# The second attention's scores in whole fp32, its query tiles copied from their bank at once, and its output tile begun in its last steps

## The chip, the cores and the metric

One core of a Trainium2 chip runs the whole program in one launch. The metric is the device time of an execution in microseconds (us); a kernel's time is the median of several executions. The profile names the engines PE (TensorE's matmuls; PEld is its weight loads), DVE (VectorE), ACT (ScalarE), POOL (GpSimd) and SP (SyncE, which issues most of the DMAs).

## What is computed

Three transformer blocks run one after the other over 512 positions of width 1024, in fp32: a block with differential attention, one with windowed attention, and a third block with convolution and forgetting attention. Between them stand gated feed-forward parts. The change touches the windowed attention, the kernel's second:

```python
q, k, v = jnp.split(h @ w_qkv, [Hq * d, Hq * d + Hkv * d], axis=-1)   # 16 query heads, 4 key heads, d = 64
q = apply_rope(q.reshape(B, S, Hq, d), cos, sin)
k = apply_rope(k.reshape(B, S, Hkv, d), cos, sin)
s = einsum('bnqhgd,bnchd->bnhgqc', q, band(k)) * d ** -0.5            # keys with |i - j| <= 128
e = exp(where(mask, s, -inf) - m);  pr = e / (sum(e) + exp(sink - m))
o = einsum('bnhgqc,bnchd->bnqhgd', pr, band(v));  return o @ w_o
# rope: (x1, x2) -> (x1 c - x2 s, x2 c + x1 s) on the halves of 32 of each head
```

## The kernel before

Activations lie with the features on the partitions: X has 8 chunks of 128 features by 512 positions. A weight slab is 128x1024. SP loads it, ACT rounds it to fp32r (`whi`, `high` at L1116), POOL subtracts to get the remainder (`wlo`, L540), and a product of an activation and a weight is made of three fp32r matmuls, hi by hi, hi by lo and lo by hi (`mm3`, L550). Four slabs are held in a ring.

The engines run programs of their own, each strictly in the order in which it is written out, and meet at semaphores. The second attention (kind 2) has 32 steps g: a pair of heads j = g // 4 and a block of 128 queries qb = g % 4. In step g:

- TensorE (`attention`, L871) makes the scores of step g + 2 (`scores`, L715: two heads side by side on the upper and lower 64 rows, three fp32r matmuls each of 256 or 384 columns, then masks added by matmuls), a quarter of the projection of a later query tile (`project_qk`, L670: 6 matmuls of 512 columns), the transposes of the probabilities of step g (L788), and in every second step the outputs of two steps. In steps with g % 4 = 0 the projection stands last, behind the outputs, since it opens a tile.
- ACT (L1285) makes the exponentials of step g + 1 (`exps`), copies the transposed probabilities out of their banks (`prob_high`), and every four steps takes an output tile out (`evacuate`). When a projection is done (g % 4 = 3) it makes the exchanged halves of the tile, four copies of 32 partitions out of the bank (`swap_halves`, L1205); one step later it rounds the rotated tile (`q_high`, L1216); two steps later it rounds the next weight slab (`replaced`, L1129), which starts POOL's split.
- DVE (L1839) takes the maxima of the scores of step g + 2 (`maxima`), normalises the probabilities of step g + 1 (`normalise`, whose last instructions are L1793), and between the two, in steps with g % 4 = 0, rotates the tile (`rope`, L1702: the tile in its bank by the cosines at L1712, the exchanged one by the sines at L1713, their sum at L1716), and in steps with g % 4 = 1 makes the rounding's remainder (`q_low`, L1737).

The query tiles 1 to 7 of the projection kq2 all go into bank 0 (`STAGE_BANKS`), which is given back by L1712. The scores of a new pair of heads, made in steps with g % 4 = 2, wait for the count `q_ready` that `q_low` raises. The last projection ends in step 23. The attention's output tiles are split into a rounded part and a remainder (`output_high` on ACT, `output_low` on DVE, in the steps that `OSPLIT` lists), and TensorE then multiplies them by the output weights (`tiles("o2", ...)`, L1020), the first two tiles chunk by chunk.

## Time and profile before

| what | us |
| --- | --- |
| median of three executions | 2061.38 (2059.04 to 2061.61) |
| the profiled execution: its time | 2063.4 |
| its span, first to last instruction | 2061.6 |
| PE busy | 2029.3 (98%) |
| DVE busy | 1182.7 (57%) |
| ACT busy | 934.1 (45%) |
| POOL busy | 904.6 (44%) |

The second attention runs from about 737 to 872 us of the span. A timeline row has the start, the time from the first start to the last end of what was merged, the engine, the line, the operation with the tensors it writes and reads, the shapes, the count, and in brackets the engine's idle time before it with what ended that. Matmuls are pipelined, so rows overlap: from one start to the next is what a matmul holds the engine for.

### The profile page before, as it was taken

Reading aid. Unit: us, or ns where it says so; the run is one execution under the profiler, and the core shown is the slowest. Engines: PE = TensorE matmul, PEld = TensorE weight load, DVE = VectorE, ACT = ScalarE, POOL = GpSimd, SP = SyncE. Lnnn points to the kernel's source line nnn. Section 1 sums busy time; section 2 is a strip of 40 time slices with the busy share of each in tenths; the row PEclk is TensorE's granted clock in tenths of the full one; section 3 lists DMA queues with packets and bytes.
Section 4 is the critical chain, followed back from the end, with each engine's and each line's share of the span. In section 5 each row is a group of like instructions: output and inputs, shape, how many; then the busy total and the mean of one; then the engine's idle time right before and its main releaser. Section 6 shows DMA issues by size and latency. Waiting matters only on the chain.

```text
span 2061.6 us, 28278 instructions
## 1 busy us (share of the span) xinstructions
PE 2029.3 (98%) x9822; PEld 1650.2 (80%) x9822; DVE 1182.7 (57%) x1714; ACT 934.1 (45%) x1479; POOL 904.6 (44%) x660
## 2 busy tenths in 40 slices
PE   9999999999999989899999999999999999999999
PEld 6777788888887877688888887878778788888887
DVE  7687857546276678757637267547787563213122
ACT  6455545434245467735434245444642544322221
POOL 5422235545446431145544556444224454454544
PEclk9999999999999999999999999999999999999999
DMA  4322123323233210122323333222113222233223
GB/s 163 95 74 76 52 72 97 107 93 99 95 101 113 88 66 32 32 92 82 109 96 102 94 98 115 91 83 84 40 52 102 82 92 92 88 107 99 95 95 110
DMA packets 52754, 183.18 MB, mean 89 GB/s; under 512 B 6576, under 2 KB 6832, under 8 KB 52656
## 3 DMA queue, kind: packets, MB, share of 16 engines
q1 hardware_dynamic: 51072, 177.76, 26.7%
q10 hardware_dynamic: 1584, 4.07, 0.5%
q8 instruction: 67, 1.10, 0.2%
q14 instruction: 31, 0.25, 0.0%
HBM read 176.04 MB, written 2.10 MB: 86 GB/s over the span
## 4 chain that ended last, share of the span: by engine, by line
issue 49%; POOL 30%; PE 19%; DVE 1%; POOLq 1%; DMA 0%; ACT 0%; SPq 0%; ACTq 0%
POOL wlo L540 30%; PE PS L548 19%; DVE AR L2260 0%; POOLq L538 0%; POOLq L535 0%; DMA raw<-in_weights 0%; DVE Blo L2264 0%; DVE AR L2258 0%; ACT Bhi L1578 0%; DVE sq L2258 0%; ACT whi L1119 0%; DVE X L1686 0%; POOLq L540 0%; SPq L503 0%; ACTq L1118 0%
## 5 line engine op out<-in xcount | busy, mean ns | idle before, releaser
L540 POOL TENSOR_TENSOR wlo<-raw,whi 128x512 fp32r<-128x512 f32 x656 | 904.4, 1401 | 1143.8 <-ACT whi L1119 1143.0
L548 PE MATMUL PS<-Bhi,whi 128*128 128x512 f32 x2352 | 927.2, 394 | 8.8 <-DVE AR L1712 7.2
L548 PE MATMUL PS<-Blo,whi 128*128 128x512 f32 x2352 | 916.7, 390 | 0.0
L548 PE MATMUL PS<-Bhi,wlo 128*128 128x512 f32 x2352 | 916.7, 390 | 0.0
L1119 ACT ACTIVATE whi<-raw 128x1024 fp32r<-128x1024 f32 x328 | 345.3, 1057 | 523.4 <-PE PS L548 437.2
L548 PEld LDWEIGHTS PS<-Bhi,whi 128*128 128x128 f32 x2352 | 442.2, 188 | 113.9 <-issue 19.4
L548 PEld LDWEIGHTS PS<-Bhi,wlo 128*128 128x128 f32 x2352 | 442.1, 188 | 93.7
L548 PEld LDWEIGHTS PS<-Blo,whi 128*128 128x128 f32 x2352 | 442.4, 188 | 90.0 <-issue 0.7
L1630 DVE TENSOR_TENSOR AR<-PS,R 128x512 f32<-128x512 f32 x170 | 115.3, 689 | 243.1 <-PE PS L548 231.4
L1686 DVE TENSOR_TENSOR X<-X,PS 128x512 f32<-128x512 f32 x88 | 60.2, 687 | 228.7 <-PE PS L548 228.0
L1906 DVE SCALAR_TENSOR_TENSOR AR<-AR,par_sb 128x511 f32<-128x511 f32 x88 | 116.8, 1327 | 9.1 <-ACT AR L1350 9.1
L1365 ACT ACTIVATE Bhi<-AR 128x512 f32 x66 | 41.8, 633 | 167.0 <-DVE AR L1922 167.0
L1909 DVE SCALAR_TENSOR_TENSOR AR<-AR,par_sb 128x511 f32<-128x511 f32 x88 | 106.8, 1214 | 12.9 <-DVE AR L1906 2.9
L1233 ACT ACTIVATE AR<-PS,nmax 128x512 f32<-128x512 f32 (+3 forms) x160 | 93.1, 590 | 41.7 <-DVE nmax L1752 40.5
L1350 ACT ACTIVATE AR<-AR,par_sb 128x512 f32<-128x512 f32 x88 | 70.9, 806 | 39.2 <-DVE AR L1630 39.2
L1639 DVE SCALAR_TENSOR_TENSOR Blo<-X,par_sb,Bhi 128x512 fp32r<-128x512 f32 x56 | 64.0, 1153 | 34.9 <-ACT Bhi L1145 27.5
L1926 DVE TENSOR_TENSOR Blo<-AR,Bhi 128x512 f32 x66 | 47.2, 715 | 62.2 <-ACT Bhi L1365 62.2
L1922 DVE TENSOR_TENSOR AR<-AR 128x512 f32<-128x512 f32 x66 | 56.0, 849 | 35.6 <-ACT AR L1361 27.2
L1646 DVE TENSOR_TENSOR acc<-acc,sq 128x512 f32<-128x512 f32 x56 | 73.2, 1307 | 0.0
L1361 ACT ACTIVATE AR<-AR 128x512 f32<-128x512 f32 x66 | 41.4, 628 | 49.3 <-DVE AR L1909 48.7
L1752 DVE TENSOR_REDUCE nmax<-PS 128x1 f32<-128x512 f32 (+3 forms) x96 | 54.9, 613 | 12.6 <-PE PS L548 12.3
L788 PE MATMUL PS<-constR,AR 128*128 128x128 f32 x368 | 56.4, 282 | 4.4 <-DVE AR L1793 4.2
(241 smaller groups left out, 1887.4 us busy)
## 6 DMA issues: line engine op xcount, KB each, us to landing
raw<-in_weights SPq DMA_DIRECT2D x328, 512.0 KB, 3.3
AR<-AR SPq DMA_DIRECT2D x56, 64.0 KB, 2.0
X<-in_xT ACTq DMA_DIRECT2D x4, 512.0 KB, 6.9
out<-X SPq DMA_DIRECT2D x8, 256.0 KB, 3.1
AR<-in_pT ACTq DMA_DIRECT2D x2, 512.0 KB, 4.3
par_sb<-in_parameters ACTq DMA_DIRECT2D x1, 314.0 KB, 8.6
AR<-in_positions ACTq DMA_DIRECT2D x1, 256.0 KB, 8.5
con_sb<-in_constants ACTq DMA_DIRECT2D x1, 198.5 KB, 8.3
```

Source lines behind the costliest of these rows:

```text
L540: ins = pool.tensor_tensor(wlo[:, j, c], raw[:, j % RAWS, c], f32(whi[:, j, c]), ALU.subtract)
L548: return pe.matmul(out, w, x, start=start, stop=stop)
L788: last = pe.transpose(PS[:, 2 + n % 2, k * P:k * P + P], source[:, k * P:k * P + P], ident)
L1119: act.activation(whi[:, slot, :], raw[:, slot % RAWS, :], ACT.Copy)\
L1233: act.activation(probs(kind)[:, 2 * (g % 2) + s, 0:nb * P], PS[:, score_bank(kind, n), 0:nb * P], ACT.Exp, bias=nmax[:, n % 4:n % 4 + 1], ...
L1350: act.activation(cv[:, 2 * pair + u, :], us[:, 2 * pair + u, :], ACT.Identity, scale=conv_w[:, l, 1, u, bass.ds(q, 1)], bias=conv_w[:, l, ...
L1630: tt(out, PS[:, bank, :], R[:, :], ALU.mult).then_inc(tile_free[bank], 1)
L1639: stt(chunks(Blo[b])[:, m, :], X[:, m, :], gain(name, col, m), f32(chunks(Bhi[b])[:, m, :]), ALU.mult, ALU.subtract).then_inc(x_split, 1)
L1646: tt(acc[:, :], acc[:, :], sq[:, slot, :], ALU.add).then_inc(sq_used, 1)
L1686: tt(X[:, m, :], X[:, m, :], PS[:, bank, :], ALU.add)\
L1906: own.step(stt(c[:, 1:T], x[:, 0:T - 1], conv_w[:, l, 0, u, bass.ds(q, 1)], c[:, 1:T], ALU.mult, ALU.add))
L1909: stt(c[:, 0:T - 1], x[:, 1:T], conv_w[:, l, 2, u, bass.ds(q, 1)], c[:, 0:T - 1], ALU.mult, ALU.add).then_inc(conv_done, 1)
```

## The change

Three things change in the second attention.

- Scores are one fp32 matmul per head (`qk32`) instead of three fp32r ones, as the third attention's are. The rounding `q_high` and the remainder `q_low` of its tiles go.
- ACT copies a projected tile out of its bank into SBUF as soon as it is done (`taken`), which gives the bank back; the exchanged halves are made from that copy, two copies right behind it and two in the next step behind the exponentials (`exchange`). DVE rotates from SBUF (`rotate`): two multiplications that carry the scale of the queries along, and a sum that writes the tile in fp32 and raises `q_ready`. It stands in steps with g % 4 = 1, where `q_low` stood.
- The output splits stand in steps 24 to 29 and 31 instead of 29 to 31, and TensorE makes the chunks 0 to 5 of output tile 0 in steps 26 to 31, behind the scores and ahead of the transposes. `tiles("o2", ...)` goes on with chunk 6.

```diff
-        OSPLIT = {29: (0, 1, 2), 30: (3, 4), 31: (5, 6)}
+        OSPLIT = {24: (0,), 25: (1,), 26: (2,), 27: (3,), 28: (4,), 29: (5,), 31: (6,)}
+        OPART = {26: 0, 27: 1, 28: 2, 29: 3, 30: 4, 31: 5}
...
-                    if kind == 3:
-                        mm(out, qk32[rows, b, 0, cols], qk32[rows, b, 1, keys], True, False)
+                    if kind > 1:
+                        mm(out, qk32[rows, b, 0, cols], qk32[rows, kb, 1, keys], True, False)
...
+                    if kind == 2 and g in OPART:
+                        pe.wait_ge(o_split, KC + OPART[g] + 1)
+                        tile("o2", 0, 0, chunks(Bhi[0]), chunks(Blo[0]), KC, first=OPART[g],
+                             end=OPART[g] + 1)
...
-            tiles("o2", KC, chunks(Bhi[0]), chunks(Blo[0]), KC, (o_split, 8))
+            tiles("o2", KC, chunks(Bhi[0]), chunks(Blo[0]), KC, (o_split, 8), begun=len(OPART))
...
+            def taken(t, stage="kq2"):
+                n = kq2_number(stage, t)
+                used(stage, 0, t, False)
+                bank, _ = tile_of(stage, 0, t)
+                act.wait_ge(q_ready, n - 1 if n >= QT0[2] + 2 else QT0[2])
+                act.activation(qraw[:, n % 2, :], PS[:, bank, :], ACT.Copy).then_inc(tile_free[bank], 1)
+
+            def exchange(t, halves, stage="kq2"):
+                n = kq2_number(stage, t)
+                bank, before = tile_of(stage, 0, t)
+                act.wait_ge(tile_free[bank], before + 2)
+                for half in halves:
+                    for to, of in ((0, 32), (32, 0)):
+                        to, of = to + 64 * half, of + 64 * half
+                        last = act.activation(swap[to:to + 32, n % 2, :], qraw[of:of + 32, n % 2, :], ACT.Copy)
+                if halves[-1] == 1:
+                    last.then_inc(swap_ready, 1)
...
                         exps(kind, g + 1)
+                    if kind == 2 and begun is not None:
+                        exchange(begun, (1,))
                     prob_high(kind, g)
-                    if kind < 3 and begun is not None:
+                    if kind == 1 and begun is not None:
                         q_high(*place_of(kind, begun))
...
                     if done is not None and kind == 2:
-                        swap_halves(PROJ[kind], done, place_of(kind, done)[0])
+                        taken(done)
+                        exchange(done, (0,))
...
+            def rotate(t, stage="kq2"):
+                n = kq2_number(stage, t)
+                b, which = place_of(2, t)[1:] if stage == "kq2" else (0, 1 - t)
+                x, y, factor = qraw[:, n % 2, :], swap[:, n % 2, :], (QSCALE, 1.0)[which]
+                dve.wait_ge(swap_ready, n - QT0[2] + 3)
+                own.step(stt(x, x, factor, rC, ALU.mult, ALU.mult))
+                own.step(stt(y, y, factor, rS, ALU.mult, ALU.mult))
+                own.wait()
+                tt(qk32[:, b, which, :], x, y, ALU.add).then_inc(q_ready, 1)
...
-                    if kind == 2 and begun is not None:
-                        rope(PROJ[kind], begun, place_of(kind, begun)[0])
-                    if kind < 3 and halfway is not None:
+                    if kind == 2 and halfway is not None:
+                        rotate(halfway)
+                    if kind == 1 and halfway is not None:
                         q_low(*place_of(kind, halfway))
```

The tiles ahead of the first step (`kq2a`, and tiles 0 and 1 of `kq2`) are copied, exchanged and rotated in the same way; tile 0 is rotated in step 0 and tile 1 in step 1.

## Rows read from the trace of the kernel before

**Rows 1.** The page: the span, and busy time, share and instructions of each engine.
```profile
span 2061.6 us, 28278 instructions
...
PE 2029.3 (98%) x9822; PEld 1650.2 (80%) x9822; DVE 1182.7 (57%) x1714; ACT 934.1 (45%) x1479; POOL 904.6 (44%) x660
```
**Rows 2.** Waits of PE, 740 to 872: us in total, times, the longest.
```profile
PE PS L548 <- DVE AR L1712: 7.2, 6, 2.4
PE PS L788 <- DVE AR L1793: 4.2, 5, 1.3
PE PS L548 <- DVE qklo L1739: 2.2, 2, 1.5
```
**Rows 3.** Timeline of PE: two waits of the start, and one period.
```profile
753.15 0.47 PE L548 MATMUL PS<-Bhi,whi 128*128 128x512 f32 x1 [2.35 <-DVE AR L1712]
...
759.20 0.39 PE L548 MATMUL PS<-qkhi 64*128 64x256 f32 x2 [1.48 <-DVE qklo L1739]
...
763.96 0.45 PE L548 MATMUL PS<-qkhi 64*128 64x384 f32 x2
...
786.32 0.47 PE L548 MATMUL PS<-Bhi,whi 128*128 128x512 f32 x1 [0.98 <-DVE AR L1712]
...
787.88 0.39 PE L548 MATMUL PS<-qkhi 64*128 64x256 f32 x2
...
790.85 0.39 PE L548 MATMUL PS<-qkhi 64*128 64x256 f32 x2
...
795.06 0.45 PE L548 MATMUL PS<-qkhi 64*128 64x384 f32 x2
795.34 0.34 PE L548 MATMUL PS<-qklo,qkhi 64*128 64x384 f32 x2
795.51 0.34 PE L548 MATMUL PS<-qkhi,qklo 64*128 64x384 f32 x2
795.69 0.29 PE L548 MATMUL PS<-constR 64*128 64x256 f32 x2
...
801.87 0.47 PE L548 MATMUL PS<-Bhi,whi 128*128 128x512 f32 x1 [0.97 <-DVE AR L1712]
```
**Rows 4.** Busy time by stretch: us; PE, PEld, DVE, ACT, POOL; granted clock; DMA.
```profile
848.00:872.00 24.00, 18.20 (x135) 12.79 (x135) 20.24 (x59) 19.69 (x62) 2.49 (x2) 0.84 0.08 23
```
**Rows 5.** Timeline of ACT: the exchanged halves of one tile.
```profile
798.62 2.39 ACT L1213 ACTIVATE AR<-PS 32x512 f32<-32x512 f32 x4
```
**Rows 6.** Timeline of DVE in the same period.
```profile
785.48 0.69 DVE L1712 TENSOR_TENSOR AR<-PS,AR 128x512 f32<-128x512 f32 x1 [0.45 <-ACT AR L1213]
...
786.81 0.69 DVE L1716 TENSOR_TENSOR AR<-AR 128x512 f32<-128x512 f32 x1
...
789.77 0.16 DVE L1764 TENSOR_TENSOR sdiff<-nmax,nsink 128x2 f32<-128x2 f32 x1
789.84 0.69 DVE L1739 SCALAR_TENSOR_TENSOR qklo<-AR,qkhi 128x512 fp32r<-128x512 f32 x1
...
793.86 1.20 DVE L1764 TENSOR_TENSOR sdiff<-nmax,nsink 128x2 f32<-128x2 f32 x1
```
**Rows 7.** Timeline of PE in the third attention: scores in fp32, then masks.
```profile
1445.53 0.92 PE L548 MATMUL PS<-qk 64*128 64x384 f32 x4
...
1446.46 0.23 PE L548 MATMUL PS<-constR 64*128 64x128 f32 x2
```
**Rows 8.** Timeline of POOL: the weight split of the same period.
```profile
792.53 2.52 POOL L540 TENSOR_TENSOR wlo<-raw,whi 128x512 fp32r<-128x512 f32 x2 [13.04 <-ACT whi L1119]
```
**Rows 9.** Timeline of PE: the first matmul of the output tiles and the seventh.
```profile
871.89 0.80 PE L548 MATMUL PS<-Bhi,whi 128*128 128x512 f32 x1
...
874.62 0.43 PE L548 MATMUL PS<-Bhi,whi 128*128 128x512 f32 x1
```
**Rows 10.** Timeline of DVE at the end: maxima of step 25, last normalisation.
```profile
850.67 0.75 DVE L1749 TENSOR_REDUCE nmax<-PS 128x1 f32<-128x256 f32 x2
...
868.49 0.61 DVE L1793 TENSOR_SCALAR AR<-AR,rinv 128x256 f32<-128x256 f32 x2
```

More of the change, by code:

```diff
@@ L458, in finished, with kq2_number @@
             return p[0] if p and p[1] == p[2] - 1 else None
+        def kq2_number(stage, t):
+            return QT0[2] + t + (2 if stage == "kq2" else 0)
         def probs(kind):
@@ L604, in tiles @@
             def tiles(stage, n, hi, lo, nk, ready, norm=None, lead=2, late=1,
-                      meanwhile=None, part=0):
+                      meanwhile=None, part=0, begun=0):
                 if ready is None:
@@ L616, in tiles @@
                             weights(s)
-                            outs.append(open_tile(stage, 0, j))
+                            outs.append(PS[:, tile_of(stage, 0, j)[0], :] if j == 0 and begun else
+                                        open_tile(stage, 0, j))
                         for k in ks:
+                            if j == 0 and k < begun:
+                                continue
                             if j == 0:
@@ L1208, in swap_halves @@
                 bank, _ = tile_of(stage, 0, t)
-                if n >= 2:
-                    act.wait_ge(rope_ready, n - 1)
                 for to, of in ((0, 32), (32, 0), (64, 96), (96, 64)):
@@ L1476, in _ @@
             for t in range(2):
-                swap_halves("kq2a", t, QT0[2] + t)
+                taken(t, "kq2a")
+                exchange(t, (0, 1), "kq2a")
             for t in range(2):
                 replaced("kq2a", t)
-            for t in range(2):
-                q_high(QT0[2] + t, 0, 1 - t)
             for q in range(2):
@@ L1485, in _ @@
             exps(2, 0)
-            swap_halves("kq2", 0, QT0[2] + 2)
-            q_high(*place_of(2, 0))
-            swap_halves("kq2", 1, QT0[2] + 3)
+            taken(0)
+            exchange(0, (0, 1))
+            taken(1)
+            exchange(1, (0,))
             attention(2)
@@ L1525, in head_square @@
             def head_square(t):
-                act.wait_ge(rope_ready, QT0[3] + t + 1)
+                act.wait_ge(rope_ready, QT0[2] + t + 1)
                 if t >= 2:
@@ L1705, in rope @@
                 b = n % 2
-                dve.wait_ge(swap_ready, n + 1 if n < 2 else n - QT0[2] + 3)
-                if n >= 2:
-                    dve.wait_ge(q_ready, n - 1)
-                    dve.wait_ge(qhi_ready, n - 1)
+                dve.wait_ge(swap_ready, n + 1)
                 tt(qraw[:, b, :], PS[:, bank, :], rC, ALU.mult).then_inc(tile_free[bank], 1)
@@ L2074, in _ @@
             for t in range(2):
-                rope("kq2a", t, QT0[2] + t)
-            for t in range(2):
-                q_low(QT0[2] + t, 0, 1 - t)
+                rotate(t, "kq2a")
             maxima(2, 0)
             normalise(2, 0)
-            rope("kq2", 0, QT0[2] + 2)
             attention(2)
@@ L2204, in head_norm @@
                 dve.wait_ge(hspread, t + 1)
-                dve.wait_ge(rope_ready, QT0[3] + t + 1)
+                dve.wait_ge(rope_ready, QT0[2] + t + 1)
                 stt(qk32[:, b, u, :], qraw3[:, u, :], gs[:, 1 + u:2 + u], PS[:, bank, :],
```

## The prediction, made before the changed kernel was run

> **What bounds the kernel now.** I read the page first: TensorE (PE) is busy for 2029.3 of 2061.6 us [rows 1], so only the 32 us in which it is idle, and the work that is given to it, can move the time. The execution took 2063.4 us in all, 1.8 more than its span; the median of the runs, 2061.38, lies 2.0 below it, so I work out a difference from the profiled one and add it to the median.
>
> Next I read TensorE's waits in the second attention alone. It has 32 steps g, four for each pair of heads; I call a step by g mod 4. Three kinds of wait carry nearly all of the idle time: 7.2 us in six waits for the first multiplication of the rotation (L1712), 4.2 us for the probabilities (L1793), 2.2 us in two waits for the low half of a query (L1739) [rows 2]. The six waits are one per tile: projection t+1 goes into the same bank 0 as projection t, and that bank is given back only when VectorE (DVE) has multiplied out of it, behind four partial copies on ScalarE (ACT). The timeline shows one period: the projection starts at 786.32 after 0.98 us of idle, and the next at 801.87 after 0.97 [rows 3], so a period is 15.55 us, of which 14.57 are work. Five such periods run from 763.96 to 841.7 (763.96 + 5 x 15.55) [rows 3]. Before them lies a start with one wait of 2.35 us, and behind them an end without projections (step 24 on), in which ACT and DVE lead and TensorE's clock fell for a time (granted 0.84 over 848 to 872) [rows 4].
>
> **The bank given back at once.** Now ACT copies the tile (128x512 out of the bank; 0.6 us, a quarter of the four partial copies' 2.39, since 512 columns go by either way) right after the projection. The first partial copy started at 798.62 [rows 5]; a whole copy there ends at 799.2 and TensorE wants the bank only after its scores, transposes and outputs of step 0, at 801.87 less 0.97, that is 800.9. Slack 1.7 us, so the wait goes: -0.98 in each of the five periods. ACT has one copy more and one rounding of the same size (q_high) less: even. Two of the four exchange copies (0.6 each, 2.39 for four [rows 5]) go behind the exponentials of the next step, which start 0.6 us earlier; the transposed probabilities of step 0 come some 0.6 later, and TensorE needs them two steps on.
>
> **What is late next.** The rotation moves from DVE's step 0 to its step 1, behind the maxima and in the place of q_low, and it must finish before TensorE's step 2, whose scores open the next pair of heads and wait for that query. In step 1 TensorE starts its scores at 787.88, DVE is through the maxima and starts q_low at 789.84, 1.96 later [rows 3, 6] (1.96 in four periods, 2.15 in one). q_low takes 0.69, and TensorE starts step 2 at 790.85, 2.97 after step 1: 0.3 us of slack. In its place stand three operations of 128x512. The old rotation is the nearest row: 785.48 to 786.81 plus 0.69, so 2.02 us [rows 6]. With 0.09 for the longer scores (below) the query is ready at 1.96 + 0.09 + 2.02 = 4.07 after the start of step 1 and TensorE arrives at 2.97 + 0.09 = 3.06: a wait of 1.0, with the signal's way 1.05. Nothing hides it: the scores of step 2 stand ahead of projection, transposes and outputs in TensorE's order, and DVE holds the normalisation of step 2 behind the rotation, which is needed after the projection only. One wait of 0.98 goes, one of 1.05 comes, a step later. Ends for it: 0 (if the three operations took under 1.0 together) and 1.25 (the period with 2.15).
>
> **Scores as whole fp32.** The third attention already does this: from the first score matmul of 384 columns, 1445.53, to the next mask, 1446.46, 0.93 us go by, in which one further pass (cc) lies [rows 7]. A pass of the present three takes 0.17 (795.34 to 795.51), so 0.76 for the new scores against 795.69 - 795.06 = 0.63 [rows 3]: +0.13. For 256 columns I take it by width, +0.09. A period has two of each: +0.44. TensorE does this on the path, since it is the bound there; nothing hides it. Ends: +0.26 (if the cc pass is counted at a third of 0.63) and +0.5. What the change saves is a q_high and a q_low per tile, which lie on engines that are not the bound.
>
> **A period** is then 14.57 + 0.44 + 1.05 = 16.06 against 15.55, +0.51; five give +2.6 us. Ends: -0.98 + 0.26 = -0.7 each (-3.6) and -0.98 + 0.5 + 1.25 = +0.8 each (+3.9).
>
> **The start** (to 763.96). The wait of 2.35 [rows 3] goes nearly whole: bank 0 is free at 749.2, when ACT has copied. But two steps on TensorE already waited 1.48 for a q_low, at 759.20 [rows 3], and there the whole rotation stands now, behind a second rotation's 2.0 in the step before. I follow DVE: maxima to 752.5, rotation to 754.5, normalisation to 755.5, maxima, then the second rotation from 756.9 at the earliest, so the query at 759.0. GpSimd (POOL) splits weights in this stretch, and DVE's operations on SBUF are held meanwhile (0.16 us became 1.20 at 793.86, while POOL worked from 792.53 to 795.05 [rows 6, 8]); the first split here begins about 755.1, the second about 758.3, and both fall on this chain, to 761.6 at the latest. TensorE starts that step between 0.2 earlier and 2.4 later than at 759.20; it had a further 0.35 wait behind, which goes. I take +0.9 for the start; ends -1.0 and +2.0.
>
> **The end** (step 24 on). The output splits move from steps 29 to 31 to one per step from 24, and six of the eight chunks of output tile 0 move into steps 26 to 31. The second frees 18 matmuls behind the attention. At present the first six of them ran from 871.89 to 874.62 [rows 9], 0.455 each, the rest at half of that (TensorE's lower level, 1.2 GHz, after a stretch in which it waited for one normalisation after the other): 2.7 + 12 x 0.227 = 5.5 us. In the attention their 0.7 per step lies where TensorE waits for DVE anyway. The first is a gain for ACT, which had three of them (1.6 us) ahead of the exponentials of step 31; but DVE has the low half of each, and in step 24 it now waits for ACT: exponentials, half an exchange, transposed probabilities and output_high end there about 850.9, so DVE starts the maxima of step 25 at 851.5, where it started at 850.67 [rows 10]. From there it has no pause: maxima 1.45, rotation 2.0, normalisation 1.1 and a split held by POOL up to 1.7, then 0.6, four steps of 2.5 + 0.6, one normalisation 1.0: 20.3, to 871.9, where the last normalisation now ends at 868.49 + 0.61 = 869.1 [rows 10]. So the outputs end 2.8 to 3.3 later, at 875.1 against 871.89, and 5.5 us of matmuls are gone: -2.3. If the clock falls again and the six remaining passes or the scores run at half speed I give back 1.4 (the six at 0.455 instead of 0.227). The chain waits on DVE for 4 us around step 25 with TensorE idle, so I take that: -0.9. Ends -3 and +1.5.
>
> **A rule against the change.** DVE's difference of two columns, 0.16 us at 789.77, took 1.20 at 793.86 and ended when POOL's second operation did, at 795.05 [rows 6, 8]. The Trainium skill, page "SBUF — State Buffer", section "SBUF: two separate sides", says that DVE operations with two SBUF inputs and GpSimd's share a port pair which one of them holds for a whole instruction. The trace agrees on the small operations. The old rotation had one such operation out of PSUM; of the new three all read two SBUF tiles. In the five periods POOL starts 4.65 after step 1, the rotation ends at 4.07, so by my sum they pass each other with 0.6 to spare; the rival below is the case that they don't.
>
> **Sum:** +2.6 (periods) + 0.1 (the longer scores of the last step before the end) + 0.9 (start) - 0.9 (end) = +2.7. 2061.4 + 2.7 = 2064.1; I say 2064. By the ends of its terms this case runs from 2061.4 - 3.6 - 1.0 - 3 = 2053.8 to 2061.4 + 3.9 + 2.0 + 1.5 = 2068.8; the ends won't all come together, and 2060 to 2068 is where I expect it.
>
> **Rivals.** (1) *The rotation isn't late* and no wait takes the place of the one removed. For it: a 0.3 us slack exists, and if the maxima were passed sooner or the two multiplications were shorter, all of 1.05 goes. Against it: all three old operations took 0.69, whatever they read, and the maxima stand ahead. Then five periods give 5 x (-0.98 + 0.44) = -2.7, the start -1.0, the end -2.3: -6, so 2055.4. (2) *Slower: the rotation runs into POOL's split.* It decides from the point where POOL starts less than 4.07 after step 1, that is 0.6 earlier than now, or the rotation that much later. POOL starts when ACT's weight copy ends, and that copy stands behind the transposed probabilities. Then two of the three operations take about 1.2 to 1.7 instead of 0.69, +1 to +2 per period: 5 x 1.4 on top of my sum, 2071. For it: it does happen in the start, by my own walk. Against it: what ACT has ahead of its weight copy does not get shorter. (3) *The clock falls in the periods*, because the new wait comes with less work before it: in the row before, TensorE's six matmuls lost 1.4 us at half clock [rows 9]; once per period +7, so 2071. Against it: waits of 0.98 per period left the clock at full speed, and the new ones are as long.
>
> **How the numbers follow.** A measurement of this kernel can tell about 0.2% (4 us) from no change: below 2057.3 is faster, above 2065.5 slower. My case 0.60 (same 0.41, slower 0.17, faster 0.02); rival 1 0.20 (faster 0.17, same 0.03); rivals 2 and 3 0.13 and 0.07 (slower 0.19, same 0.01). Together faster 0.19, same 0.45, slower 0.36. The range for 8 in 10 takes in half of rival 1 and half of rivals 2 and 3: 2055 to 2071.
>
> **What would show it.** In the changed profile the wait for L1712 is gone from TensorE's list, and waits for the new rotation's last addition stand there, seven or more, near 1.05 each, at the scores of step 2; the period is 16.06. Score pairs of 384 take 0.76 to the mask. The first matmul behind the last outputs comes some 3 us later after step 24 than now, and is one of chunk 6. I am wrong if the period is under 15.2 (rival 1), if the rotation's additions take over 1 us in the periods (rival 2), or if the granted clock falls between 764 and 842 (rival 3).

## The result, and the profile after

The changed kernel takes 2067.64 us in the median of 8 runs, the kernel before 2061.41 on the same chip: the ratio of their runs is 1.0033, 95% interval 1.0025 to 1.0042. By the medians that is 6.2 us slower, 3.6 above the forecast of 2064 and inside its range. The profiled execution took 2066.82 us, 1.8 more than its span.

On the page TensorE (PE) is busier by 1.8 us and the span is longer by 3.4 than in [rows 1]:

```profile
span 2065.0 us, 28121 instructions
...
PE 2031.1 (98%) x9758; PEld 1647.3 (80%) x9758; DVE 1168.9 (57%) x1704; ACT 935.7 (45%) x1479; POOL 904.4 (44%) x660
```

The span understates the loss: before the attention the profiled execution of after was 0.9 ahead, and behind it the one of before lost 1.1 on balance, with a clock fall near 1496 us (granted clock 0.83 over 1490 to 1500; 1.00 in after). So I measure between four rows that both kernels have (called the ledger below): the last update of X ahead of the attention, the sink difference of steps 6 and 26, and the first update of X from output tile 0. VectorE (DVE) rows of before:

```profile
716.57 0.69 DVE L1952 TENSOR_TENSOR X<-X,PS 128x512 f32<-128x512 f32 x1
...
769.33 0.16 DVE L1764 TENSOR_TENSOR sdiff<-nmax,nsink 128x2 f32<-128x2 f32 x1
...
847.08 0.16 DVE L1764 TENSOR_TENSOR sdiff<-nmax,nsink 128x2 f32<-128x2 f32 x1
...
883.81 0.69 DVE L1686 TENSOR_TENSOR X<-X,PS 128x512 f32<-128x512 f32 x1 [9.28 <-PE PS L548]
```

and of after:

```profile
715.66 0.69 DVE L1994 TENSOR_TENSOR X<-X,PS 128x512 f32<-128x512 f32 x1
...
774.01 0.16 DVE L1806 TENSOR_TENSOR sdiff<-nmax,nsink 128x2 f32<-128x2 f32 x1
...
853.87 0.16 DVE L1806 TENSOR_TENSOR sdiff<-nmax,nsink 128x2 f32<-128x2 f32 x1
...
888.40 0.69 DVE L1721 TENSOR_TENSOR X<-X,PS 128x512 f32<-128x512 f32 x1 [3.97 <-PE PS L554]
```

After minus before at the four: -0.91, +4.68, +6.79, +4.59. So the start costs 5.6, twenty steps (five periods) cost 2.1, the end gives back 2.2: +5.5 for the attention, of the 6.2 that the runs show. The start alone is nearly the whole loss.

TensorE's waits, 740 to 880 us (who waited, for what, by which line; us in total, times, the longest), against [rows 2]:

```profile
PE PS L554 <- DVE qk L1758: 14.6, 7, 5.8
PE PS L798 <- ACT pt L1290: 1.0, 1, 1.0
PE PS L798 <- DVE AR L1835: 0.5, 1, 0.5
```

The bank's wait is gone, and so are q_low's and most of those for the probabilities. In their place stand seven waits for the rotation's last addition (L1758), 14.6 us. TensorE's timeline has them (start, length; in brackets the idle time before and who ended it), the counterpart of [rows 3] and [rows 9]:

```profile
754.56 0.88 PE L798 MATMUL PS<-constR,AR 128*128 128x128 f32 x6 [0.51 <-DVE AR L1835]
761.20 1.22 PE L554 MATMUL PS<-qk 64*128 64x256 f32 x4 [5.76 <-DVE qk L1758]
...
768.40 0.92 PE L554 MATMUL PS<-qk 64*128 64x384 f32 x4
...
780.09 0.70 PE L554 MATMUL PS<-qk 64*128 64x256 f32 x4 [0.99 <-DVE qk L1758]
...
791.95 0.70 PE L554 MATMUL PS<-qk 64*128 64x256 f32 x4
...
796.06 0.70 PE L554 MATMUL PS<-qk 64*128 64x256 f32 x4 [1.01 <-DVE qk L1758]
...
861.50 1.22 PE L554 MATMUL PS<-qk 64*128 64x256 f32 x4 [3.77 <-DVE qk L1758]
...
881.89 0.47 PE L554 MATMUL PS<-Bhi,whi 128*128 128x512 f32 x1
```

One wait of 5.76 in the start, five of about 1.0 in the periods (796.06 less 780.09: a period is 15.97), one of 3.77 at the end. The four score matmuls of 256 columns behind the longest waits take 1.22 where those of the periods take 0.70: they ran at the lower of TensorE's two clock levels. Busy time by stretch shows the same (us; PE, PEld, DVE, ACT, POOL; granted clock; DMA), the counterpart of [rows 4]:

```profile
744.00:764.00 20.00, 13.72 (x74) 10.15 (x73) 14.73 (x35) 13.38 (x34) 5.68 (x4) 0.83 0.25 80
...
858.00:869.00 11.00, 7.50 (x39) 5.43 (x40) 9.73 (x23) 7.10 (x23) 2.62 (x2) 0.69 0.15 49
758.00:769.00 11.00, 7.80 (x38) 5.73 (x38) 6.04 (x14) 2.42 (x10) 2.60 (x2) 0.56 0.29 95
```

Over 758 to 769 the clock is 0.56, so nearly all of that stretch is at 1.2 GHz; before it was 1.00 there.

What holds the rotation in the start is on DVE and on GpSimd (POOL), the counterparts of [rows 6] and [rows 8]. DVE:

```profile
756.01 1.20 DVE L1806 TENSOR_TENSOR sdiff<-nmax,nsink 128x2 f32<-128x2 f32 x1
757.13 0.68 DVE L1755 SCALAR_TENSOR_TENSOR AR<-AR 128x512 f32<-128x512 f32 x1
757.73 1.75 DVE L1756 SCALAR_TENSOR_TENSOR AR<-AR 128x512 f32<-128x512 f32 x1
759.51 1.63 DVE L1758 TENSOR_TENSOR qk<-AR 128x512 f32<-128x512 f32 x1
...
793.99 0.68 DVE L1755 SCALAR_TENSOR_TENSOR AR<-AR 128x512 f32<-128x512 f32 x1
794.60 0.69 DVE L1756 SCALAR_TENSOR_TENSOR AR<-AR 128x512 f32<-128x512 f32 x1
795.32 0.69 DVE L1758 TENSOR_TENSOR qk<-AR 128x512 f32<-128x512 f32 x1
```

POOL:

```profile
754.59 2.60 POOL L546 TENSOR_TENSOR wlo<-raw,whi 128x512 fp32r<-128x512 f32 x2 [11.57 <-ACT whi L1133]
757.51 3.09 POOL L546 TENSOR_TENSOR wlo<-raw,whi 128x512 fp32r<-128x512 f32 x2 [0.33 <-ACT whi L1133]
...
796.75 2.70 POOL L546 TENSOR_TENSOR wlo<-raw,whi 128x512 fp32r<-128x512 f32 x2 [13.27 <-ACT whi L1133]
```

In the start two of the second rotation's three operations lie under POOL's second split, and it takes 4.0 us (757.13 to 761.14); in the period the rotation is over at 796.01, 0.7 ahead of the split, and takes 2.0.

### The profile page after: what moved, and what is told of

The parts are those of the page before. It is cut to its first block, busy times and chain, and to the rows that moved or that the text cites. A ratio compares the mean times of both kernels' runs of the same rounds, so it can differ in the third digit from the quotient of the medians.

```text
span 2065.0 us, 28121 instructions
## 1 busy us (share of the span) xinstructions
PE 2031.1 (98%) x9758; PEld 1647.3 (80%) x9758; DVE 1168.9 (57%) x1704; ACT 935.7 (45%) x1479; POOL 904.4 (44%) x660
## 4 chain that ended last, share of the span: by engine, by line
issue 49%; POOL 30%; PE 19%; DVE 1%; POOLq 1%; DMA 0%; ACT 0%; SPq 0%; ACTq 0%
POOL wlo L546 30%; PE PS L554 19%; DVE AR L2299 0%; POOLq L544 0%; POOLq L541 0%; DMA raw<-in_weights 0%; DVE Blo L2303 0%; DVE AR L2297 0%; ACT Bhi L1613 0%; DVE sq L2297 0%; ACT whi L1133 0%; DVE X L1721 0%; POOLq L546 0%; SPq L509 0%; ACTq L1132 0%
## 5 line engine op out<-in xcount | busy, mean ns | idle before, releaser
L1290 ACT ACTIVATE pt<-PS 128x256 f32<-128x256 f32 (+3 forms) x96 | 37.0, 437 | 51.4 <-PE PS L798 50.9
```

## The experiments

Two questions stood open: is the start, as the ledger says, the loss, and which of its causes (POOL's split, DVE's order, the clock) makes it; and what the three parts of the change are worth each. All differences are between medians, against the kernel before as it ran beside the variant on the same chip, unless another is named; where two variants are compared that ran on different chips, each goes by its own difference. The ledger (start, five periods, end, by the four rows above, against the profiled execution of before, us) of all kernels:

| kernel | start | periods | end | attention | by the runs |
|---|---|---|---|---|---|
| after | +5.6 | +2.1 | -2.2 | +5.5 | +6.2 |
| rotate_first | +5.6 | -3.3 | -1.5 | +0.8 | +1.2 |
| split_later | +2.3 | +4.8 | -1.8 | +5.3 | +6.0 |
| end_as_before | +5.2 | +2.1 | -0.5 | +6.7 | +7.1 |
| scores_only | -0.1 | +1.3 | -2.4 | -1.1 | -0.2 |
| copy_at_once | +2.5 | +0.7 | -0.1 | +3.1 | +5.3 |
| start_early | +3.0 | -3.3 | -0.7 | -0.9 | +0.7 |
| start_early_split_later | +0.3 | -1.6 | -1.4 | -2.7 | -0.2 |
| first_end_as_before | +5.5 | -3.3 | -1.3 | +1.0 | +1.5 |
| start_in_order | -0.1 | +2.0 | -2.8 | -0.9 | +0.5 |
| start_and_first | +1.3 | -3.3 | -0.9 | -2.9 | -2.2 |
| start_first_end_later | +1.4 | -3.3 | -3.8 | -5.7 | -6.6 |
| start_first_end_before | -0.3 | -3.3 | -0.6 | -4.1 | -0.8 |

The ledger is one execution each; by the runs all kernels but one come out 0 to 3 us worse than their ledger. I take that for differences between executions, in the rest of the program and in the clock's falls (single runs of one kernel spread over 2 to 8 us, and the execution of before that the ledger measures against was 2.0 slower than its median), but I did not trace it.

**rotate_first.** In the periods the rotation goes ahead of the maxima, from which it needs nothing.

```diff
+                    if kind == 2 and halfway is not None and g > 1:
+                        rotate(halfway)
                     if g + AHEAD[kind] < steps:
                         maxima(kind, g + AHEAD[kind])
...
-                    if kind == 2 and halfway is not None:
+                    if kind == 2 and halfway is not None and g <= 1:
                         rotate(halfway)
```

> The changed kernel, with the rotation put ahead of the maxima in steps 5, 9, ... 25 (the start, steps 0 and 1, stays). My theory: each period's wait for the query (1.01 us at the scores of step 2) comes from the rotation standing behind maxima that wait for TensorE's scores of step 1. The exchanged halves are there 0.5 us after step 1 begins, so the rotation ends at 2.5 and the wait goes: periods 14.97, five times -1.0, and 1 to 2 us less in the end: 2061 to 2062.5 against 2067.6. Rival: DVE has too much to do in step 1 in any order, and the wait moves to the transposes of step 1 or 2 (L1835): period 15.9 to 16, 2066.5 to 2068.

Measured: 2061.21 against 2060.04, ratio 1.0006 (0.9997 to 1.0016). TensorE's waits, 738 to 885:

```profile
PE PS L554 <- DVE qk L1758: 8.4, 2, 5.8
PE PS L798 <- ACT pt L1290: 1.0, 1, 1.0
```

The five waits of the periods are gone, two of the seven are left (5.76 in the start, 2.65 at the end); a period is 14.90 (14.97 expected), and over 765 to 845 TensorE is busy for 80.00 of 80 us. The periods went from +2.1 to -3.3 in the ledger. So the new wait was DVE's order and nothing deeper: the theory held.

**split_later.** The first two replaced weight slabs, whose rounding on ScalarE (ACT) starts POOL's splits, are rounded in steps 2 and 3 instead of 0 and 1.

```diff
-                    if kind == 2 and halfway is not None:
-                        replaced("kq2", halfway)
+                    late_slab = halfway if g > 1 else None
+                    if g in (2, 3):
+                        late_slab = g - 2
+                    if kind == 2 and late_slab is not None:
+                        replaced("kq2", late_slab)
```

> The changed kernel, with the rounding of the first two replaced weight slabs (and so POOL's splits of them) moved from steps 0 and 1 to steps 2 and 3. My theory: the wait of 5.76 us at the start comes from POOL holding the second rotation's operations (1.75 and 1.63 us instead of 0.69) and the maxima's before it (1.20 instead of 0.16), and the long wait then lets TensorE's clock fall. Without POOL there the query is ready 3 us earlier, the wait is 2.5 to 3, and the half clock behind it (2.4 us) goes if the wait is short enough: 2062 to 2064.5. Rival: the chain of two rotations and two maxima is what is late, POOL only happens to lie there: wait 5 or more, 2066.5 to 2068.

Measured: 2065.99, ratio 1.0027 (1.0016 to 1.0038), above the 2062 to 2064.5 expected. TensorE's waits of the start and the first period (the rotation's last addition is L1761 in this kernel):

```profile
757.61 1.23 PE L554 MATMUL PS<-qk 64*128 64x256 f32 x4 [2.50 <-DVE qk L1761]
777.62 1.22 PE L554 MATMUL PS<-qk 64*128 64x256 f32 x4 [2.00 <-DVE qk L1761]
```

With no split beside it the second rotation took 2.0 us and the start's wait fell from 5.76 to 2.50: the hold by POOL is shown, and so is that it is not the whole wait. But the splits now lay on the first period (the normalisation's two multiplications took 1.46 at 773.05 instead of 0.75), its wait doubled, and the score matmuls behind either wait still took 1.22, at half clock. What the start gained (3.2) the first period lost (2.7). The expectation had the mechanism and missed where the splits would go.

**end_as_before.** The third part undone: the chunks' splits and output tile 0 as before.

```diff
-        OSPLIT = {24: (0,), 25: (1,), 26: (2,), 27: (3,), 28: (4,), 29: (5,), 31: (6,)}
+        OSPLIT = {29: (0, 1, 2), 30: (3, 4), 31: (5, 6)}
-        OPART = {26: 0, 27: 1, 28: 2, 29: 3, 30: 4, 31: 5}
+        OPART = {}
```

> The changed kernel without its third part: the output splits in steps 29 to 31 again, and no chunk of output tile 0 inside the attention. My theory: the third part frees 5.5 us of matmuls behind the attention and delays the attention's last outputs by some 3, net -2.2, so without it the kernel is slower still: 2069 to 2070.5. Rival: by making DVE wait for ACT in steps 24 on, it costs what it gives: 2067 to 2068. Second rival: it is the loss: 2064 or less.

Measured: 2067.16 against 2060.04, ratio 1.0032 (1.0020 to 1.0045), so +7.1 where after has +6.2: the third part is worth 0.9, with intervals that overlap. That lies between the theory's 1.4 to 2.9 and the rival's nothing (-0.6 to +0.4). In the ledger the two kernels' ends lie 1.7 apart (-2.2 and -0.5); why it is so little the later runs of the end show.

**scores_only.** The kernel before with the scores in fp32 and the rotation written straight to the queries and keys, out of the bank and in its old place.

```diff
-                    if kind == 3:
+                    if kind > 1:
...
-                    dve.wait_ge(qhi_ready, n - 1)
+                    _, place, which = place_of(2, t) if stage == "kq2" else (0, 0, 1 - t)
+                    factor = (QSCALE, 1.0)[which]
+                    tt(qraw[:, b, :], PS[:, bank, :], rC, ALU.mult).then_inc(tile_free[bank], 1)
+                    own.step(stt(swap[:, b, :], swap[:, b, :], factor, rS, ALU.mult, ALU.mult))
...
+                    stt(qk32[:, place, which, :], qraw[:, b, :], factor, swap[:, b, :],
+                        ALU.mult, ALU.add).then_inc(q_ready, 1)
```

> The kernel before with the scores in whole fp32 alone: the old rotation out of the bank at its old place, its last operation carrying the scale and writing the fp32 tile, no rounding and no remainder. My theory: 0.42 us per period and somewhat less in start and end, against which the two waits for a remainder (2.2 us) go: 2061.4 + 2.1 + 0.6 - 1.5 = 2062.6, with the waits of 0.98 for the bank unchanged in the trace. Rival: the fp32 scores are the loss by themselves: 2066 to 2068.

Measured: 2059.86 against 2060.04, ratio 0.9998 (0.9989 to 1.0008). The theory had +1.2, the rival +5 to +7: by the total, the scores are no part of the loss. In the periods they cost what was forecast (+1.3): a period is 15.81 (before 15.55), with a wait of 0.86 in it for the bank, so its work is 14.95, 0.38 more than before's 14.57. The end gives it back (-2.4).

**copy_at_once.** The second part alone: the copy out of the bank and the exchange from it, all in one step; the rotation reads the copies and stands where it stood, queries and scores are as before.

```diff
+            def taken(stage, t, n):
...
+                act.activation(qraw[:, n % 2, :], PS[:, bank, :], ACT.Copy).then_inc(tile_free[bank], 1)
+                act.wait_ge(tile_free[bank], before + 2)
+                for to, of in ((0, 32), (32, 0), (64, 96), (96, 64)):
+                    last = act.activation(swap[to:to + 32, n % 2, :], qraw[of:of + 32, n % 2, :], ACT.Copy)
+                last.then_inc(swap_ready, 1)
```

> The kernel before with one part of the change alone: each tile is copied out of its bank at once and exchanged from the copy (all four copies of the exchange in the step that ends the tile), the rotation stays in the next step as before, the queries and keys stay split and the scores stay three products, the end stays as before. Theory (the bank was what the waits of the kernel before were for, and the rotation's place is what turned them into new ones): TensorE's six waits on line 1712 (7.2 us, rows 2) are gone, no new wait over 0.5 us takes their place in the periods, and the time is 4 to 7 us below the kernel before (about 2053.5 to 2056.5 if that is 2060.5). Rival (the fifth ScalarE copy of a tile, about 0.6 us, delays the exponentials or the split of the query as much as the bank's release brings): a wait of 0.8 to 1.2 us a period stays, put down to another line, and the time is within 2 us of the kernel before.

Measured: 2065.03 against 2059.72, ratio 1.0025 (1.0015 to 1.0035): slower, where I had expected 4 to 7 us faster. The theory fell; the rival had the mechanism, as the rows below show, but its time (within 2 us) was passed by 3. TensorE's waits, 738 to 885:

```profile
PE PS L548 <- DVE qklo L1753: 4.5, 7, 1.3
PE PS L788 <- DVE AR L1807: 3.9, 5, 1.3
PE PS L548 <- ACT AR L1244: 3.1, 2, 1.6
```

For the bank one wait of 0.70 is left, in the start (750.23, for the copy at L1221); none is in the periods. ACT's timeline of one tile shows what took its place:

```profile
783.57 0.61 ACT L1221 ACTIVATE AR<-PS 128x512 f32<-128x512 f32 x1
784.20 2.55 ACT L1224 ACTIVATE AR<-AR 32x512 f32<-32x512 f32 x4
786.77 0.58 ACT L1244 ACTIVATE AR<-PS,nmax 128x384 f32<-128x384 f32 x1
...
787.35 0.57 ACT L1244 ACTIVATE AR<-PS,nmax 128x384 f32<-128x384 f32 x1
```

and TensorE's shows the scores of steps 1 and 2:

```profile
787.51 0.38 PE L548 MATMUL PS<-qkhi 64*128 64x256 f32 x1
...
788.06 0.38 PE L548 MATMUL PS<-qkhi 64*128 64x256 f32 x1
...
791.65 0.39 PE L548 MATMUL PS<-qkhi 64*128 64x256 f32 x2 [0.54 <-DVE qklo L1753]
```

Five copies, 3.2 us, stand where four took 2.4 [rows 5], and the exponentials behind them start at the end of the five. That makes two waits. The second head's scores of step 1 may start only when the second exponential is done, at 787.92: they start 0.55 behind the first head's (787.51, 788.06), where before the two start together (787.88 [rows 3]); the list of waits does not have this one. And the rotation, the high half on ACT and the low half on DVE follow each other behind the copies, so that TensorE waits 0.54 for q_low. Together they are 1.09 where the bank's wait was 0.98, and a period is 15.70 for 15.55. Giving the bank back sooner was worth nothing here, with a fifth copy ahead of the exponentials and the chain through q_high and q_low behind it; which of the two would have been enough was not separated. Of the 5.3 us the ledger shows 3.1; where the rest lies I did not settle.

**start_early.** rotate_first, with both rotations in step 0, ahead of the normalisation of step 1.

```diff
-                    if kind == 2 and halfway is not None and g <= 1:
-                        rotate(halfway)
+                    if kind == 2 and g == 0:
+                        rotate(0)
+                        rotate(1)
```

> rotate_first with one more move: in the start of the attention both rotations stand in step 0 (the second no longer behind the maxima of step 3), ahead of the normalisation of step 1. Theory (the 5.76 us wait of the start is the second rotation running beside GpSimd's splits, and the clock fall behind it, 7.2 us of work where the kernel before took 4.76, is a consequence of that wait): the second rotation ends by 756.5 us on that trace's scale instead of 760.7, the start's waits add up to 2 to 3.5 us, the clock does not fall there, and the time is 4 to 6 us below rotate_first, thus 3 to 5 us below the kernel before. Rival (the clock falls in the start whatever the length of the waits there, since the fp32 scores and the waits together thin the work out): the waits shrink by 2.5 to 3.5 us but the fall stays, and the time is 2.5 to 3.5 us below rotate_first.

Measured: 2060.37, ratio 1.0001 (0.9992 to 1.0010), 0.5 under rotate_first by the two differences (+0.7 and +1.2). The 5.76 is gone, but the wait was handed to the normalisation behind the rotations:

```profile
757.12 1.54 PE L798 MATMUL PS<-constR,AR 128*128 128x128 f32 x6 [4.49 <-DVE AR L1835]
```

and behind it the clock fell as before (0.87 over 745 to 772, 0.81 in rotate_first). Both theory and rival had wanted 2 us more: a wait that DVE's order makes is not removed by letting another operation take it.

**start_early_split_later.** start_early and the later rounding of split_later together.

> start_early with the first two replaced slabs rounded in steps 2 and 3, so that GpSimd's splits begin after both rotations. Theory (what held the second rotation is GpSimd's split beside it: 1.75 and 1.63 us for operations of 0.69): the second rotation takes about 2.1 us, ends by 755.6 us on the scale of rotate_first's trace, the start's waits are 1.5 to 2.5 us, and the wait that split_later grew in the first period (0.99 to 2.00 us) does not come back, as the rotation now runs ahead of the maxima: 1 us below start_early to level with it. Rival (the splits, moved onto the first period, hold its rotation there, as in split_later): a wait of 1 us or more in the first period and a time 1 to 2 us above start_early.

Measured: 2059.51, ratio 0.9999 (0.9990 to 1.0008). The start's wait is 2.45, so 2.0 of start_early's 4.49 were POOL's, and its clock 0.94 over 745 to 772; the first period has one of 0.86 for the rotation and one of 0.44 for the normalisation. Within the theory's "1 us below to level", but the start still waits for a normalisation that stands behind two rotations.

**first_end_as_before.** rotate_first with the third part undone, as in end_as_before.

> rotate_first with the third part undone (the splits of the output's chunks and the output tile as in the kernel before). It sizes that part where nothing else is late. Theory (the part is worth what the ledger of the two traces shows, the output tile's first chunks done 2.2 us earlier against the last step): 2 us above rotate_first. Rival (end_as_before against the changed kernel: 0.9 us, of which the clock falls in the end take the rest): 0.5 to 1.2 us above rotate_first, with the clock fall of the end short or gone in this kernel.

Measured: 2061.19, ratio 1.0008 (0.9999 to 1.0017): +1.5 where rotate_first has +1.2. So here the third part is worth 0.3 by the runs, under the rival's 0.5 and the theory's 2.

**start_in_order.** The changed kernel, with its start alone in the order in which its operands come: the first rotation ahead of the attention, the second behind the normalisation of step 1.

```diff
             normalise(2, 0)
+            rotate(0)
             attention(2)
...
-                    if kind == 2 and halfway is not None:
+                    if kind == 2 and halfway is not None and g > 1:
                         rotate(halfway)
...
                         normalise(kind, g + 1)
+                    if kind == 2 and g == 0:
+                        rotate(1)
```

> The changed kernel with its start alone reordered on VectorE: the first rotation ahead of the attention's maxima, the second in step 0 behind the normalisation of step 1 (in the changed kernel they are in steps 0 and 1, the second behind the maxima of step 3); the periods and the end are the changed kernel's. Theory (the start is the term that the prediction mis-sized: the second rotation came late enough to run beside GpSimd's splits, and the long wait pulled the clock down): the second rotation ends by 754.2 us on the scale of start_early's trace, ahead of the first split, no wait of the start is over 0.8 us, the clock does not fall there, and of the 5.2 us that the start cost about 5 come back: 0.5 to 2.5 us above the kernel before, 4 to 5.5 us below the changed kernel. Rival (the loss only moves, since TensorE's work of the first periods is short of the replaced slabs or of the exponentials): waits of 2 us or more appear in steps 2 to 6 and the time stays within 2.5 us of the changed kernel.

Measured: 2060.12 against 2059.64, ratio 1.0000 (0.9991 to 1.0009): 5.7 under after's +6.2, a little more than the theory's 4 to 5.5. DVE:

```profile
747.45 0.69 DVE L1755 SCALAR_TENSOR_TENSOR AR<-AR 128x512 f32<-128x512 f32 x1 [1.99 <-ACT AR L1244]
...
752.58 0.75 DVE L1835 TENSOR_SCALAR AR<-AR,rinv 128x384 f32<-128x384 f32 x2
753.35 0.69 DVE L1755 SCALAR_TENSOR_TENSOR AR<-AR 128x512 f32<-128x512 f32 x1
...
754.68 0.69 DVE L1758 TENSOR_TENSOR qk<-AR 128x512 f32<-128x512 f32 x1
```

The second rotation ends at 755.37, and POOL's first split starts at 755.17 in the same trace. TensorE's waits in the start are 0.70 for ACT's exponentials and 0.92 and 0.79 for a normalisation, the clock is 1.00 over 745 to 772, and in the ledger the start's 5.6 is gone whole. This settles the main question: what the change lost, it lost in the start, by the place of two rotations on DVE. (Both were moved at once; how much each gives was not separated.) The periods still wait 1.01 each, as in after.

**start_and_first.** start_in_order and rotate_first together.

> start_in_order with the rotation ahead of the maxima in every later step, too (as in rotate_first). Theory (start and periods are separate losses that add): no waits at the scores in the start or in the five periods, 5.5 to 7 us of waits and half clock gone against rotate_first's start, the end as in rotate_first (1.0, 2.65 and a clock fall): 4 to 5 us below rotate_first, thus 2.5 to 4.5 us below the kernel before. Rival (the clock falls in the start with any wait, as in start_early_split_later with 2.45 us): 2 us above that, level with the kernel before to 2 us below.

Measured: 2057.43 against 2059.64, ratio 0.9989 (0.9980 to 0.9998). The periods' gain comes on top, 2.7 of the 5.3 that the ledger has between +2.0 and -3.3; the profiled execution had the start's waits as in start_in_order (0.69, 0.92, 0.80), but the clock fell behind them for a time (0.94 over 745 to 772), which is the +1.3 in the ledger. It is the slowest of the kernel's 11 executions (2061.91, 4.5 above their median). Between theory (-2.5 to -4.5) and rival (0 to -2).

**start_first_end_later.** start_and_first, with the third part begun one step later.

```diff
-        OSPLIT = {24: (0,), 25: (1,), 26: (2,), 27: (3,), 28: (4,), 29: (5,), 31: (6,)}
+        OSPLIT = {25: (0,), 26: (1,), 27: (2,), 28: (3,), 29: (4,), 31: (5, 6)}
-        OPART = {26: 0, 27: 1, 28: 2, 29: 3, 30: 4, 31: 5}
+        OPART = {27: 0, 28: 1, 29: 2, 30: 3, 31: 4}
```

> start_and_first with the end begun a step later: the output's chunks are split from step 25 on (not 24) and the output tile is begun in step 27 (five chunks of it ahead of the end instead of six). In the traces the last rotation (step 25) stood on VectorE behind the first chunk's low half, which waited 1.4 us for ScalarE's high half, and TensorE's scores waited 2.65 us for that rotation; behind it the clock fell. Theory: the last rotation ends 1.9 us sooner, the 2.65 us wait shrinks to under 1 us, the clock falls later or for less, and the time is 1 to 3 us below start_and_first. Rival (the clock falls in the end whatever the waits, since the projections are over and little is left for TensorE): the wait shrinks, the fall stays, and the time is within 1 us of start_and_first.

Measured: 2053.09 against 2059.64, ratio 0.9967 (0.9955 to 0.9979): faster than either kernel, and 4.3 under start_and_first, more than the 1 to 3 expected. In start_and_first DVE's timeline at the last tile reads

```profile
848.53 0.69 DVE L1879 TENSOR_TENSOR Blo<-AR,Bhi 128x512 fp32r<-128x512 f32 x1 [1.41 <-ACT Bhi L1370]
849.14 0.69 DVE L1755 SCALAR_TENSOR_TENSOR AR<-AR 128x512 f32<-128x512 f32 x1
...
850.46 0.69 DVE L1758 TENSOR_TENSOR qk<-AR 128x512 f32<-128x512 f32 x1
```

and in start_first_end_later

```profile
846.23 0.69 DVE L1755 SCALAR_TENSOR_TENSOR AR<-AR 128x512 f32<-128x512 f32 x1
...
847.56 0.69 DVE L1758 TENSOR_TENSOR qk<-AR 128x512 f32<-128x512 f32 x1
```

The first chunk's low half, which waited 1.41 for ACT, no longer stands ahead of the last rotation; TensorE's wait for it is 0.71 instead of 2.65, and the end gives 3.8 in the ledger instead of 0.9. The rival had one thing right: the clock still fell in the end (0.79 over 842 to 858; 0.76 in start_and_first).

**start_first_end_before.** start_and_first with the third part undone, to tell the freed rotation from the early chunks.

> start_and_first with the third part undone (the splits of the output's chunks and the output tile as in the kernel before). Beside start_first_end_later it sizes the third part where the last rotation is not held. Theory (in start_and_first the part gives with its early chunks what it takes by holding the last rotation; begun a step later it only gives): within 1.5 us of start_and_first (thus 1 to 4 us below the kernel before), and 2 to 4.5 us above start_first_end_later. Rival (what start_first_end_later gained was the freed rotation alone, the early chunks are worth nothing): level with start_first_end_later, 5.5 to 7.5 us below the kernel before.

Measured: 2059.46 against 2060.21, ratio 0.9998 (0.9989 to 1.0007). The last rotation is free here, too (TensorE's wait for it is 0.71), and the kernel is still 5.8 above start_first_end_later by the runs, 3.2 by the ledger's ends. So the rival fell: the early chunks are worth 3 to 6 us where they hold nothing, more than the 2 to 4.5 I expected by the runs, and nearly nothing (0.3 to 1.5) where they hold the last rotation.

## Why the prediction came out as it did

The range held the time and the direction of the forecast was right, but the likeliest case (2064, within 0.2%) was not the one that came: it is slower by 0.33%, which had 0.36. That the range held owes something to luck: the start came out far beyond its own ends (-1.0 to +2.0), the end gave back 1.3 more than I took, and the range's upper part stood there for rivals 2 and 3, which did not come where I had put them.

- **The bank's wait goes, a wait for the rotation comes.** Right, and to the size: 15.97 for a period against 16.06 predicted, waits of 0.99 to 1.01 against 1.05. In the trace the rotation begins 2.04 after TensorE's step 1 (793.99 less 791.95; predicted 2.05), takes 2.02 (2.02), and TensorE arrives 3.10 after it (796.06 - 1.01 - 791.95; 3.06). The work of a period is 14.96, 0.39 above before's (predicted 0.44; scores_only: 0.38). Five periods cost +2.1 for a predicted +2.6.
- **The start** is the term that was mis-sized: +0.9 predicted, ends -1.0 and +2.0, measured +5.6 by the ledger of the four rows and 5.7 by start_in_order. My walk along DVE had the right order: second rotation from 756.9 at the earliest (757.13), held by POOL's second split, query at 761.6 at the latest. It was there at 761.14 in an execution 0.9 ahead of before, so at 762.0 on the scale of the walk, 0.4 past its latest. I wrote that both splits fall on this chain and then took a middle between held and not held, though no row spoke for the middle. That is 2.8 us: the scores began at 761.20, 2.0 later than [rows 3] have them and 0.8 more by the head start (at the first scores ahead of the steps after was 0.81 ahead). Another 2.4 lies behind them: from those scores to those of step 3, 761.20 to 768.40, TensorE took 7.2 us at the lower clock for what took 4.76 before at the full one, a wait of 0.35 among them (759.20 to 763.96 [rows 3]). The sum had no term for the clock there. Of the rest, some 0.4, 0.24 lies between the scores of step 3 and the second row of the ledger (5.61 us for 5.37). I had priced a clock fall as a rival for the periods, and the reason that I gave against it, that waits of 1 us leave the clock alone, does not hold for the start, where my own walk had a wait of up to 3.9 us (the 1.48 of 759.20 and 2.4 more).
- **Rivals 2 and 3** came true together, but in the start and not in the periods, where I had put them. In the periods POOL's split starts 4.80 after step 1 (796.75; predicted 4.65) and the rotation is over at 4.06; the clock stayed at full speed over 764 to 842 but for the tail of the start's fall. Rival 1 did not come: the rotation is late. rotate_first shows how little was missing, one swap on DVE.
- **The end**: -0.9 predicted, -2.2 in the ledger; by the runs the third part is worth 0.9 (end_as_before). The first matmul behind the last outputs is one of chunk 6, as said, at 881.89; before, chunk 6 came at 871.89 + 5.5 = 877.4, so 4.5 later while step 24 was 6.7 later. The walk through step 24 was right (DVE waits 1.41 for ACT's high half, then come the maxima at 858.30, at 850.67 in [rows 10], then the rotation); the last outputs come 3.2 later, as it says. The wait of 3.77 (4 us in my sum) and the clock fall behind it (0.69 over 858 to 869) came, too, but the 1.4 that I gave back for the clock was not due: the fall was over by 869, and the six matmuls that were left ran at full clock (881.89, each 0.23 behind the last; 1.00 over 869 to 885). Without the 1.4 my sum is -2.3.
- **The scores**: right; off by 0.05 a period. The 0.76 to the mask that I had named as a sign can't be seen, since the masks' row starts while the scores' runs (848.26 and 848.72); by the next matmul behind them a pair of 384 takes 1.08 (848.26 to 849.34) against 0.97 before (841.70 to 842.67).

What is shown: the place of the rotations makes the loss (start_in_order, rotate_first), the hold by POOL is part of it (split_later), the scores by themselves are not (scores_only). The 2.4 us at the lower clock were not separated by a run of their own; where the wait of 5.76 went whole (start_in_order), they went with it, and behind the 2.50 of split_later the fall stayed. Not settled is why the same waits (0.70, 0.92, 0.79) were followed by a fall in start_and_first and start_first_end_later and not in start_in_order and start_first_end_before.

The Trainium skill, page "SBUF — State Buffer", section "SBUF: two separate sides", says that GpSimd and VectorE, in operations with two SBUF inputs, contend for one port pair which is held for a whole instruction. The trace agrees: under the second split two operations of 0.69 took 1.75 and 1.63 (757.73, 759.51), while the maxima, which read a bank, kept their 0.75 under the first split of the same stretch.

## What to carry to other kernels

Giving a buffer back sooner moves the wait to the next link of the chain behind it: to the rotation in the changed kernel, to the exponentials and q_low in copy_at_once, which came out 5.3 us slower. It can pay only when the next link is moved out of the way as well. How much, the record leaves open: with both waits gone (start_first_end_before: the first two parts in the better order, without the third) the periods of the ledger gain 3.3 us, but the runs show 0.8, which is not clear of nothing. When an operation moves into a later step, walk the start and the end of the loop with the same care as a period: there the neighbours are others, and one long wait costs the clock on top. And an in-order engine should take its work in the order in which operands arrive and results are wanted: three edits of order and place (start_in_order, rotate_first, the end begun later) turned 6.2 us lost into 6.6 us gained.

## What the runs showed of the hardware

- In the start of the attention the clock fell behind waits of very different length: behind one of 4.49 or 5.76 us each time (five kernels; granted clock 0.81 to 0.87 over 745 to 772), behind 2.2 to 2.5 in three kernels (scores_only, split_later, start_early_split_later; 0.87 to 0.94), behind 0.70 and 1.56 in copy_at_once (0.94), and behind three waits of 0.7 to 0.9 in two kernels of four (0.94, and 1.00 in the other two). Before, 2.35 and 1.48 with the three-product scores left it at 1.00.
- DVE's multiplication of the probabilities by a column (L1835), 0.75 us for two, took 2.86 under a split of POOL (758.06 in start_in_order), though it reads one tile only; two such took 1.46 under part of one (773.05 in split_later).
- A whole copy out of the bank (128x512) takes ACT 0.61, one exchange copy of a quarter of the partitions 0.64 from SBUF (784.20: 2.55 for four) and 0.60 from the bank [rows 5]: 32 partitions took as long as 128, so one more copy is a quarter more.
